# The rows of the second last expert pass: stored and gathered instead of spread by products

## The reference, cut to what matters

```
for grp in range(4):                       # each token belongs to one group
    hid = silu(t @ w_gate[grp]) * (t @ w_up[grp])      # 4 experts of 256 each
    out = out + (hid * combine[:, grp]) @ w_down[grp]
x = x + out
return rmsnorm(x, final_norm_g)
```

## Time and profile before

| what | value |
|---|---|
| median of 3 runs | 701.88 us (701.83 to 702.55) |
| the profiled execution's own time | 701.97 us |
| its span, first to last instruction | 699.9 us |
| PE busy | 678.7 us (97%) |
| DVE busy | 282.1 us (40%) |
| ACT, POOL busy | 144.3 us (21%), 78.9 us (11%) |
| mean granted TensorE clock | 0.993 of full |

### The profile page before, as it was taken

The page is one execution under the profiler, slowest core; times in us unless marked ns, Lnnn a source line. Parts: engine busy times, 40 slices in busy tenths (PEclk is TensorE's granted clock), DMA queues, the critical chain, the costliest instruction groups (busy, mean ns, idle before and its releaser), DMA issues.

```text
span 699.9 us, 8436 instructions
## 1 busy us (share of the span) xinstructions
PE 678.7 (97%) x3398; PEld 332.1 (47%) x3398; DVE 282.1 (40%) x669; ACT 144.3 (21%) x308; POOL 78.9 (11%) x106
## 2 busy tenths in 40 slices
PE   7999999999999999999999999999999999999993
PEld 4644445453557665444444555555564333333331
DVE  3107599935244665313120312323335821212156
ACT  3011251003053454211011122221111110101113
POOL 3000082312020000000000000000001110110063
PEclk9999999999999999999999999999999999999997
DMA  8803140301136513300009410630169999999673
GB/s 296 309 0 121 62 178 1 121 1 62 61 120 186 181 61 121 120 1 0 1 1 377 178 45 1 240 121 35 55 210 329 312 365 388 370 381 387 238 233 127
DMA packets 69939, 111.90 MB, mean 160 GB/s; under 512 B 5648, under 2 KB 43780, under 8 KB 69900
## 3 DMA queue, kind: packets, MB, share of 16 engines
q1 hardware_dynamic: 65724, 96.16, 39.7%
q0 software_dynamic: 4176, 15.21, 5.9%
HBM read 101.90 MB, written 9.46 MB: 159 GB/s over the span
## 4 chain that ended last, share of the span: by engine, by line
PE 90%; DMA 4%; DVE 2%; ACT 1%; POOL 1%; issue 1%; SPq 0%; DVEq 0%; POOLq 0%; ACTq 0%
PE bank L1931 19%; PE bank L2200 16%; PE bank L1806 11%; PE bank L2278 8%; PE bank L1835 5%; PE bank L1941 5%; PE bank L2288 2%; PE bank L1977 2%; PE bank L2308 2%; PE bank L2166 2%; DMA W<-y_dram,A 2%; PE bank L1963 2%; PE bank L1788 1%; PE bank L2144 1%; PE bank L2153 1%; PE bank L2049 1%
## 5 line engine op out<-in xcount | busy, mean ns | idle before, releaser
L2200 PE MATMUL bank<-W,n_sb 128*128 128x512 f32 x256 | 114.3, 596 | 0.0
L1931 PE MATMUL bank<-hT,W 128*128 128x512 f32 x240 | 104.5, 593 | 0.0
L1806 PE MATMUL bank<-W,A 128*32 128x512 f32 x672 | 84.8, 594 | 1.5 <-DVE A L1175 1.5
L2200 PEld LDWEIGHTS bank<-W,n_sb 128*128 128x128 f32 x256 | 47.3, 190 | 52.4 <-issue 52.3
L1931 PEld LDWEIGHTS bank<-hT,W 128*128 128x128 f32 x240 | 45.2, 190 | 56.1 <-issue 55.8
L2278 PE MATMUL bank<-hT,W 128*128 128x512 f32 x128 | 56.1, 592 | 0.0
L1441 DVE SCALAR_TENSOR_TENSOR A<-A,pc 128x511 f32<-128x511 f32 (+29 forms) x60 | 51.6, 860 | 2.0
L698 POOL TENSOR_TENSOR rstd<-ss,mhalf 128x1 f32<-128x1 f32 x14 | 7.7, 550 | 357.8 <-DVE ss L1068 199.0
L1806 PEld LDWEIGHTS bank<-W,A 128*32 128x32 f32 x672 | 23.1, 110 | 49.6 <-issue 47.6
L2278 PEld LDWEIGHTS bank<-hT,W 128*128 128x128 f32 x128 | 24.3, 190 | 28.1 <-issue 27.5
L1835 PE MATMUL bank<-Dn,A 128*32 128x512 f32 x264 | 36.3, 595 | 0.0
(11 more groups left out here) (311 smaller groups left out, 844.1 us busy)
## 6 DMA issues: line engine op xcount, KB each, us to landing
W<-in_w_gate_dram SPq DMA_DIRECT2D x14, 1024.0 KB, 5.4
W<-in_w_up_dram SPq DMA_DIRECT2D x14, 1024.0 KB, 10.1
Dn<-in_w_down_dram SPq DMA_DIRECT2D x11, 1024.0 KB, 14.6
W<-in_w_in_dram SPq DMA_DIRECT2D x5, 2048.0 KB, 8.6
W<-in_w_xkv_dram SPq DMA_DIRECT2D x4, 2048.0 KB, 7.9
hT<-in_w_down_dram SPq DMA_DIRECT2D x5, 1024.0 KB, 12.6
y_dram<-A POOLq DMA_DIRECT2D x10, 512.0 KB, 7.3
W<-in_w_out_dram SPq DMA_DIRECT2D x2, 2048.0 KB
```

The lines of the kernel that those rows point to most:

```text
L1806: mm = nc.tensor.matmul(PS[2 + b][r, :], xgT[:, b, c, r], gu_at[GU_HOME[e]][:, c, :], start=c == 0, stop=c == DC - 1)
L1931: mm = nc.tensor.matmul(bank[0:w, 0:n], lhs, src[:, c, 0:n], start=c == 0, stop=c == DC - 1)
L2200: mm = nc.tensor.matmul(PS[(k + (2 if base else 0)) % 4][:, :], src[:, c, t * P:(t + 1) * P], W[:, (n_load + n) % SLOTS, c, :], start=firs ...
```

## The change

`LATE` goes from 2 to 1. That makes `ZERO_ROW` 1408 instead of 1280, `y_dram` 128 rows longer, the store loop and the `y_stored` waits one pass longer (eleven stores: six of even passes, five of odd), and leaves one table, one `turn_late` and one `late_turned`. Pass 10 is now a pass like the first ten: DVE copies its second half, POOL stores it, and its rows are gathered. Pass 11 alone is spread by products, 8 of them. In `down_pass` the wait of the last pass on `y_act` alone becomes the wait of all others, on `y_act` for bank 5 and on `y_dve` for bank 6. The eight gathers keep their number and size.

```
--- before.py
+++ after.py
@@ -69,7 +69,7 @@
 TAKEN = [e for g in range(NG) for e in (4 * g, 4 * g + 3, 4 * g + 1, 4 * g + 2)]
 OVER_PARTS = -(-(S - CAP) // P)
 OVER_ROWS = EX * P
-LATE = 2
+LATE = 1
 ZERO_ROW = (NP - LATE) * P
 
 
@@ -257,8 +257,8 @@
         zero8 = srow[:, 564:572]
         limit = srow[:, 572:592].rearrange("p (s k) -> p s k", k=4)
 
-        spreadT = states[:, 0:16, :].rearrange("p a b -> p (a b)").rearrange("p (l t r) -> p l t r", l=LATE, t=ST)
-        spread_w = A[:, 10240:11264].rearrange("p (l n) -> p l n", l=LATE)
+        spreadT = states[:, 0:8 * LATE, :].rearrange("p a b -> p (a b)").rearrange("p (l t r) -> p l t r", l=LATE, t=ST)
+        spread_w = A[:, 10240:10240 + S * LATE].rearrange("p (l n) -> p l n", l=LATE)
         late_tmp = A[:, 11536:12048].rearrange("p (t r) -> p t r", t=ST)
         first_pick = A[:, 11536:12048].rearrange("p (t r) -> p t r", t=ST)
         ov_y = xg[:, 1]
@@ -678,14 +678,14 @@
                                                  in_offset=bass.IndirectOffsetOnAxis(ap=ov_token[:, 0:1], axis=0)).then_inc(ov_xg, 16)
 
                 pool.wait_ge(ov_stored, 16 * OVER_PARTS * EX)
-                pool.wait_ge(y_stored[0], 16 * (NP - LATE) // 2)
-                pool.wait_ge(y_stored[1], 16 * (NP - LATE) // 2)
+                for k in range(2):
+                    pool.wait_ge(y_stored[k], 16 * len(range(k, NP - LATE, 2)))
                 pool.wait_ge(slots_done, 4)
                 gather_rows((ov_slot[:, 0], ov_slot[:, 1]), y_dram)
             with pool.Else():
 
-                pool.wait_ge(y_stored[0], 16 * (NP - LATE) // 2)
-                pool.wait_ge(y_stored[1], 16 * (NP - LATE) // 2)
+                for k in range(2):
+                    pool.wait_ge(y_stored[k], 16 * len(range(k, NP - LATE, 2)))
                 pool.wait_ge(slots_done, 2)
                 gather_rows((slot1, slot2), y_dram[0:ZERO_ROW + 1, :])
             for t in range(ST):
@@ -1309,8 +1309,8 @@
                     y_half(p - 1)
                 if p == 1:
                     late_rows()
-                if p in (3, 5):
-                    late_turned(p // 2 - 1)
+                if p == 3:
+                    late_turned(0)
 
             def add_row(k, t, w):
                 dve.wait_ge(fin_in[t][k], 16)
@@ -1823,10 +1823,7 @@
                 for e in sorted(set(pass_experts(p))):
                     down_loaded(pe, e)
                 for n, left in enumerate((y_act, y_dve)):
-                    if p == NP - 1:
-
-                        pe.wait_ge(y_act, p + n)
-                    elif p:
+                    if p:
 
                         pe.wait_ge(left, p)
                     for k in range(2):
@@ -1874,8 +1871,8 @@
 
                     pe.wait_ge(ht_sb, p)
                 turn_hidden(p % 2, ht_ps)
-                if p in (2, 4):
-                    turn_late(p // 2 - 1)
+                if p == 2:
+                    turn_late(0)
             down_pass(NP - 1)
 
             pe.wait_ge(over_done, 1)
```

## The result

| | before | after |
|---|---|---|
| median (range) of 4 runs each | 702.21 us (701.83 to 702.77) | 711.52 us (711.41 to 711.95) |
| profiled execution's own time | 701.97 | 711.95 |
| its span | 699.9 | 710.2 |
| PE busy | 678.7 (97%) | 671.6 (95%) |

The ratio is 1.0133, 95% interval 1.0116 to 1.0151: 9.3 us slower by the medians, 9.98 by the two profiled executions. Predicted were 10.4 more and 712.3 us, range 709.9 to 714.0.

What follows compares the result with a forecast made beforehand. The end was taken to be set by copy, store, gathers and DVE's adds after pass 9, not by TensorE. Terms 10.80 + 0 + 0 + 0 - 0.44 + 0 = +10.36 us on 701.97 gave 712.3 us, range 709.9 to 714.0.

Steps and rivals of the forecast that it cites:

- The rows are ready 10.80 us later: Gathers wait for all stores; the last is now pass 10's, not pass 9's: +10.80 us on the path.
- The store adds nothing: Pass 10's 3.21 us store takes pass 9's place on the path: 0, with ends 0 and +4.1 us.
- The gathers: Same eight indirect gathers, same size and cap of three, 19.44 us from first issue to last landing: 0 change.
- The zero row: Rival: repeated zero-row reads are a hot spot, halving them saves 1.1 to 2.7 us, 709.6 to 711.2; chance 0.08.
- The products are hidden: Eight of sixteen spreading products go, 7.00 us of TensorE work; the gathers hide it, so 0.
- The second table: Four transposes on TensorE at 587.17 go with the dropped table: -0.44 us, ends 0 and -0.44.
- The copy on DVE: ACT's 0.59 us copy of pass 10 becomes DVE's of 0.69 us; last pass's second bank waits for it: 0.
- gathers at the store's pace: Rival: gathers take 3.2 us each once TensorE and copies are quiet, 7.2 us less, 705.1; chance 0.03.
- a slow store: Rival: pass 10's store is slow, +4.1 us, 716.4; chance 0.04.
- TensorE as the bound: Rival: TensorE sets the end at the spreading products, 7.0 + 0.44 us less, 694.5; chance 0.01.
- The signs: Expected in the trace: DVE's copy near 669.5, last store near 670.7, first gather near 674.7, last landing near 694.2.

Runs made afterwards that it cites:

- store10_last: Changed kernel with pass 10's rows stored to an unread buffer, that store issued and waited for behind the eight gathers: 701.56 us, ratio 0.9994 to the kernel before.
- wait11_rows10: Changed kernel with pass 10's rows stored to an unread buffer, slots from 1280 reading the zero row, gathers still waiting for that store: 711.59 us, ratio 1.0143.
- after_nozero: Changed kernel with slots at or behind row 1408 turned into slot minus 1408, so 112 zero-row reads go to 112 different rows: 711.95 us, ratio 1.0140.
- after_hot512: Changed kernel with every slot over 512 cut to 512, so 702 of 1024 reads go to one row: 712.29 us, ratio 1.0147.
- after_16products: Changed kernel with each of the 8 spreading products made twice: 711.16 us, ratio 1.0138.

## Why the prediction was right, point by point

1. *The rows are ready 10.80 us later.* Shown: 669.97 - 659.11 = 10.86, made of 10.80, the 0.44 saved and the 0.50 of the first load. store10_last takes just this away, with pass 10's rows left out as in wait11_rows10, and gets the loss back. What I had not seen is that two things hold the gathers, the wait for the landing and POOL's own order; I named the wait, and its removal alone gave 1.7 us where I had expected 10.2. The sum doesn't depend on it, since both hang on the same copy.
2. *The store adds nothing.* 3.20 against 3.21 us. Right.
3. *The gathers.* 19.36 against 19.44 us. Right, if with some luck: the same eight gathers took 18.0 to 19.8 us in the traces with the cap of three. The zero row, at 0.08, was the likeliest rival: it fell by after_nozero and after_hot512. In my sum the time from landing to first gather was taken as it stood (0.79 us); it fell to 0.26 by the order of two waits, which none of the steps held. It is the largest miss of the sum, 0.53 us, and in the profiled execution it was made good by chance by the 0.50 of the first load: the spans differ by 10.3 us, with 10.36 forecast.
4. *The products are hidden.* 7.1 us less on TensorE and none in the time; the opposite, 6.9 us more, shows none either. I had TensorE done at 680.8; it was 682.3. 0.5 is the late start, 0.8 of the rest a wait that I had overlooked: with one table left, the first product waits for ACT's copies of pass 11, where before pass 10's product was made meanwhile. Hidden with the rest.
5. *The second table.* The gate and up products of pass 5 start at 587.61 in before (587.17 and 0.44) and at 587.67 after, with the start 0.50 late: 0.44 gained. Right; no experiment undid it alone.
6. *The copy on DVE* started when its bank was ready and nothing waited for it. Right.

The rivals: gathers at the store's pace did not come (19.36 us); a slow store did not (3.20); TensorE as the bound is excluded by after_16products. The signs came too: DVE's copy at 669.97, the last store at 671.22 and the first gather at 674.68, with the last landing at 694.04, each within 0.6 us of where I had it. The measured 711.5 is 0.8 under the forecast: 0.5 is the miss in point 3, and the rest lies within what runs of the same kernel differ.

## What to carry to other kernels

An engine that is busy for 97% of the span may still not be what ends it: find where the chain of waits leaves it for the last time, and weigh a trade of its work against another's only by the distance between the two lines at the end. The distance can be measured by adding work: here 6.9 us more on TensorE cost 5.2, so TensorE stood some 1.6 us short of being last, and less work on it could win nothing. And a wait taken away for an experiment proves nothing as long as the engine's own order holds the same instruction at an earlier one: look at what stands ahead in its queue.

## What the runs showed of the hardware

- An indirect gather of 128 rows of 4 KB takes 4.3 to 6.4 us from issue to landing with up to three under way, the plain store of the same 512 KB 2.9 to 3.2 with nothing else moving. The Trainium skill (DMA: Bandwidth & Descriptors, anatomy of one DMA on the GpSimd path) has a fixed 2.0 us and 436 GB/s; for 512 KB that gives an estimate of 3.2 us, right for the store and too little for every gather here.
- POOL spends 0.94 to 1.00 us on issuing a gather, and up to 1.94 when it begins beside one of DVE's adds with two SBUF inputs: in the changed kernel the fourth is issued at 679.49, 0.23 us behind the add that starts at 679.26, and takes 1.86. In all 112 issues of the fourteen traces the rule is the same: one that begins with 0.27 us or more of such an add left ends 0.80 to 0.82 us after the add. Beside DVE's product with one input in a PSUM bank (L1293 of before) the four issues that met it took 0.94. The Trainium skill (SBUF — State Buffer, section on who interferes with whom) says that a DVE instruction with two SBUF inputs contends with a GpSimd instruction that reads SBUF. The rows agree with that (1.05 us of the add were left, 0.9 us were lost), if issuing a gather counts as such a read, which no run here tests.
- Of two waits in a row on POOL, the next issue came 0.26 us after the landing if the first was the one that blocked, 0.8 if the second was (three traces or more of each). Why was not tried.
